# Expert layers of a two-block transformer: nine buffers for picked rows in place of eleven, and another place and moment for the last four query blocks

## The reference, cut to what matters

```python
def peer_ffn(x, norm_g, q_w, sub_keys, u, v):      # T = 256 tokens, D = 1024
    h = rmsnorm(x, norm_g).reshape(T, D)
    q = (h @ q_w).reshape(T, PEER_HEADS, 2, PEER_HALF)          # 8 heads, 2 halves of 128
    s = jnp.einsum('thcd,ckd->thck', q, sub_keys)               # 128 keys for each half
    s1, i1 = lax.top_k(s[:, :, 0], 16)
    s2, i2 = lax.top_k(s[:, :, 1], 16)
    # all 256 sums of pairs, the best 16, their expert numbers idx and softmax gates
    ...
    a = jnp.einsum('nd,nhkd->nhk', hb, u[ib])                   # each token: 8 heads x 16 experts
    w = gb * jax.nn.gelu(a, approximate=False)
    return jnp.einsum('nhk,nhkd->nd', w, v[ib])
```

## Time and profile before

| | us |
|---|---|
| median of 3 runs | 2757.41 |
| lowest, highest | 2756.09, 2761.15 |
| the profiled execution, its own time | 2753.48 |
| span of the profile (first to last instruction) | 2751.7 |
| POOL waits for PE ahead of gathers, whole span | 512.5 (319 waits) |
| DVE waits for gathers, whole span | 383.6 (314 waits) |

### The profile page before, as it was taken

How to read it: one execution, slowest core, us unless ns; L and a number is a source line. 1 busy time by engine, 2 the same in 40 slices (tenths; PEclk the granted TensorE clock), 3 DMA queues, 4 the chain that set the end, 5 groups by cost and what they waited for, 6 DMA issues and landing times.

```text
span 2751.7 us, 32201 instructions
## 1 busy us (share of the span) xinstructions
PE 2464.5 (90%) x10416; PEld 1675.6 (61%) x10416; DVE 1902.5 (69%) x3840; ACT 1178.2 (43%) x2586; POOL 857.9 (31%) x700
## 2 busy tenths in 40 slices
PE   8999999999899999998899777779888898787788
PEld 7888788888778878986444333334764444233234
DVE  7885588888668875655667767666567676766664
ACT  4446744544574456563333322333453333333334
POOL 0005400000230026664333333443433333333443
PEclk9999999999999999999999999889999999988999
DMA  6554355555425544448999999999549999999995
GB/s 212 188 177 138 128 194 186 180 191 184 148 90 189 190 153 138 154 153 353 419 416 418 417 418 409 418 413 395 178 153 419 419 419 418 413 419 415 413 415 239
DMA packets 141953, 783.39 MB, mean 285 GB/s; under 512 B 15873, under 2 KB 16385, under 8 KB 76289
## 3 DMA queue, kind: packets, MB, share of 16 engines
q0 software_dynamic: 73728, 536.90, 47.2%
q1 hardware_dynamic: 65360, 237.44, 25.7%
q10 hardware_dynamic: 2736, 7.46, 0.9%
HBM read 780.69 MB, written 1.05 MB: 284 GB/s over the span
## 4 chain that ended last, share of the span: by engine, by line
PE 47%; DMA 24%; DVE 9%; ACT 7%; issue 7%; POOL 6%; POOLq 0%; ACTq 0%; SPq 0%; DVEq 0%
DMA arena<-experts,arena 24%; PE ps L703 11%; PE ps L681 6%; PE ps L682 6%; PE ps L683 6%; PE ps L704 5%; PE ps L1283 5%; PE ps L1286 5%; POOL ring_lo L387 4%; DVE arena L2687 2%; POOL arena L2804 2%; ACT row L1887 2%; ACT arena L1880 1%; ACT L1878 1%; DVE ring_lo L387 1%
## 5 line engine op out<-in xcount | busy, mean ns | idle before, releaser
L2687 DVE SCALAR_TENSOR_TENSOR arena<-arena,ps 128x1024 f32<-128x1024 f32 x512 | 617.5, 1220 | 385.1 <-DMA arena<-experts,arena 383.6
L1283 PE MATMUL ps<-arena,row 128*128 128x512 f32 x1024 | 570.1, 640 | 207.5 <-ACT row L1887 207.5
L2804 POOL DMA_INDIRECT arena<-experts,arena x512 | 483.4, 944 | 772.2 <-PE ps L1286 512.5
L1286 PE MATMUL ps<-arena,row 128*128 128x512 f32 x1024 | 553.9, 623 | 0.0
L381 ACT ACTIVATE ring_hi<-ring 128x1024 fp32r<-128x1024 f32 x416 | 437.7, 1058 | 177.7 <-PE ps L683 140.3
L703 PE MATMUL ps<-hT,ring_hi 128*128 128x512 f32 x1408 | 503.4, 400 | 3.4 <-DVE hT L2208 3.2
L1283 PEld LDWEIGHTS ps<-arena,row 128*128 128x128 f32 x1024 | 197.5, 201 | 487.3 <-ACT row L1887 279.3
L387 POOL TENSOR_TENSOR ring_lo<-ring,ring_hi 128x1024 fp32r<-128x1024 f32 x143 | 346.3, 2432 | 282.3 <-ACT ring_hi L381 261.6
L704 PE MATMUL ps<-hT,ring_lo 128*128 128x256 f32 x1408 | 395.8, 281 | 0.0
L1286 PEld LDWEIGHTS ps<-arena,row 128*128 128x128 f32 x1024 | 206.7, 202 | 269.0 <-issue 269.0
L387 DVE TENSOR_TENSOR ring_lo<-ring,ring_hi 128x1024 fp32r<-128x1024 f32 x273 | 331.9, 1239 | 20.5 <-ACT ring_hi L381 19.9
(11 more groups left out here) (341 smaller groups left out, 3553.8 us busy)
## 6 DMA issues: line engine op xcount, KB each, us to landing
ring<-stream SPq DMA_DIRECT2D x424, 512.0 KB, 3.4
arena<-experts,arena POOLq DMA_INDIRECT x512, 13.2
row<-rows_in ACTq DMA_DIRECT2D x11, 512.0 KB, 4.9
arena<-stream SPq DMA_DIRECT2D x8, 512.0 KB, 5.0
queries_in_ring_hi<-stream SPq DMA_DIRECT2D x8, 512.0 KB, 6.2
queries_in_w<-stream SPq DMA_DIRECT2D x4, 512.0 KB, 7.5
queries_in_h_lo<-stream SPq DMA_DIRECT2D x4, 512.0 KB, 5.4
x<-x_in SPq DMA_DIRECT2D x1, 1024.0 KB, 4.8
```

The costliest lines, as they stand in the source:

```text
L1283: lower = pe.matmul(ps[:, 2 * tb, :], diag, v[:, 0:HALF], start=first, stop=end)
L1286: pe.matmul(ps[:, 2 * tb + 1, :], diag, v[:, HALF:D], start=first, stop=end)\
L2687: last = dve.scalar_tensor_tensor(u, u, 1.0, h, ALU.mult, ALU.mult, accum_out=R["a"][:, n % 2, k:k + 1])
L2804: pool.indirect_dma_start(R["held"][:, g % HELD, :], None, experts, bass.IndirectOffsetOnAxis(ap=idx[:, n % 2, k:k + 1], axis=0))\
```

## The change

The ring of buffers for picked rows has nine places in place of eleven; pick g then waits until pick g - 9 is freed. The two places given up hold 4096 elements, which is the size of four query blocks. A tensor `last_queries` of that size lies at the end of the arena, and query blocks 12 to 15 have their place there and no longer in `ring_hi`. SP issues their loads together with those of blocks 2 and 3, after the wait for the mixer's last output and ahead of blocks 4 to 7, and no longer behind these and behind the waits on `used`. The rest of the program is the same: the same picks, products and order on PE, DVE, ACT and POOL.

```diff
-HELD = 11
+HELD = 9
...
-                       ("held", (HELD, EXPERT)))
+                       ("held", (HELD, EXPERT)), ("queries", (SLOTS, BLK)))
...
-        queries_in_w, queries_in_ring_hi = plain("queries_in_w", w_at, 2, BLK), plain("queries_in_ring_hi", ring_hi_at, SLOTS, BLK)
+        queries_in_w = plain("queries_in_w", w_at, 2, BLK)
+        last_queries = region(SPACE - SLOTS * BLK, SLOTS, BLK)[0]
...
-            return queries_in_ring_hi[:, b % SLOTS, :]
+            return last_queries[:, m - 3 * SLOTS, :]
...
-                        for early in (2, 3):
+                        for early in (2, 3, *range(3 * SLOTS, SUBS)):
                             sp.dma_start(raw(b + early), stream[b + early]).then_inc(raw_loaded(b + early), 16)
-                    if m < SLOTS or m // SLOTS == 2:
+                    if m // SLOTS != 1:
                         b += 1
                         continue
-                    if m < 2 * SLOTS:
-                        who, own = SPLIT[b - 2 * SLOTS][1:]
-                        sp.wait_ge(lo_ready[who], own + 1)
-                    else:
-                        sp.wait_ge(used, AT[f"peer{l}_q"] - SLOTS + m % SLOTS + 1)
+                    who, own = SPLIT[b - 2 * SLOTS][1:]
+                    sp.wait_ge(lo_ready[who], own + 1)
```

## The result

The changed kernel takes 2808.07 us (median of four runs, 2799.28 to 2810.93) where the kernel before, run beside it, takes 2757.07 (2756.09 to 2761.15): ratio 1.0175, 95% interval 1.0163 to 1.0187, so 51 us slower. The forecast was slower, 2795, with 2773 to 2820 around it. Its sign and place hold; its sum is 13 us low, and that is the net of larger errors.

The account below looks back on a forecast made before the run. The gathers' DMA queue was taken to bound both expert layers. Late pick 9 +37, second-order waits +2, query loads -0.7 and sub-keys +1 gave +39, taken as +38: 2795 us, range 2773 to 2820.

Parts of the forecast that it names:

- What bounds the kernel: Both expert layers, 656 us each: gathers set the pace at 2.49 us a pick, and empty-queue time is lost for good.
- Part 1, which gather is late, and for whom: Expert layers: pick 0's release now lets pick 9 go, not pick 11; pick 9 is late in 24 units.
- Part 1, by how much pick 9 is late: Expert layers: with 7.5 us per landing, 1.27 us on average in late units; +37 us taken, bounds 13 and 43.
- prediction's own last sign: Expert layers: the forecast is wrong if pick 0's release to pick 9's landing is not about 7.5 us.
- Rival A: Expert layers: the queue's stock covers two fewer buffers, needing an empty-queue price under 5.3 us; 2757 us, chance 0.05.
- they follow at the full rate: Unit 4 of layer 0: picks 10 and 11 follow late pick 9 at 2.49 us each, adding no further loss.
- Part 2: Expert layers: second-order waits at pick 1 and PE's lower clock after stalls, 0 to 15 us together, counted as 2.
- rival C: Expert layers: PE's lower clock after stalls delays later picks, another 1 us in twenty-four units; 2819 us, chance 0.14.
- Part 3: SP's query loads: early landing gains 0.7 us; sub-keys possibly late in layer 1 cost +1, bounds 0 and 4.
- rival D: Start of layer 1: first gather late by 3 us, beside the forecast and inside its range, with no separate chance.
- the +1: Start of layer 1: sub-keys landing behind the early query loads delay the first gather, counted +1 us, bounds 0 and 4.
- Rival B: Expert layers: a landing into an empty queue takes 6.6 us, losing 13 to 20 us; 2770 to 2778 us, chance 0.14.

Follow-up runs that it names:

- e3: Kernel before with all eleven buffers, but pick 9 of every unit waits as if there were nine: 2784.9 us, ratio 1.0099.
- e4: Kernel before with ten buffers in place of eleven: 2762.8 us, ratio 1.0014.
- e7: Kernel before with eight buffers, query blocks where they were: 2927.5 us, ratio 1.0621.
- e8: Kernel before, unedited, profiled once more in a single execution: 2760.3 us.
- e1: Kernel before with nine buffers alone, query blocks 12 to 15 left in ring_hi and loaded as before: 2803.7 us, ratio 1.0169.
- e11: Changed kernel with a unit's gates worked out on DVE between the last two dots of group 0, not behind them: 2779.3 us, ratio 1.0069.
- e2: Changed kernel run again, unedited: 2806.9 us, ratio 1.0177.
- e9: Kernel before, eleven buffers, with the next unit's expert numbers made ahead of the dots of group 2: 2756.4 us, ratio 0.9993.

## Why the prediction was right, and where it wasn't

*What bounds the kernel.* Right. The gathers' queue sets both stretches; every microsecond of the loss is in them, and a loss in the queue is not made good.

*Part 1, which gather is late, and for whom.* Right, and the core of it. The release of pick 0 lets pick 9 go; 27 units are dry there (24 were forecast), none before. e3 shows it by that wait alone, e4 and e7 that the place moves with the ring.

*Part 1, by how much pick 9 is late.* Forecast +37, with bounds 13 and 43. Measured as idle engines, +30 in the stretches, and as longer intervals ahead of pick 9, +27; about 9 of these, in the first unit of each layer, go with the late first release that e8 shows in the kernel before as well. The inputs were off in two directions. A dry pick 9 is used 5.5 to 7.3 us after its issue, 6.2 on average: less than 7.5, and less than the lowest landing of the earlier trace rows. By the prediction's own last sign, a landing about 7.5 us after the release, this input was wrong. But the release comes later: from the start of the dot of pick 3 to the issue that waits for it, 9.7 us on average, against 8.6 in the profile before and 9.2 in the second one (e8). The two partly cancel, and that is luck: neither was foreseen.

The Trainium skill's estimate ("DMA: Bandwidth & Descriptors", the anatomy of one DMA on the gpsimd path) of 4.4 us was too low here as well: from the issue to the last packet of a dry pick 9 the trace has 5.6 us on average and 5.05 at least. Rival A, which needed that price, is refuted by the result and by e1.

*Part 1, "they follow at the full rate".* This is the step that failed. The gathers behind a dry one come 3.1, 2.9 and 2.7 us apart, not 2.49: 0.6 + 0.4 + 0.2 = 1.3 us in each of 27 units (with unrounded means), 35 us. It shows as packets that take longer, +26 us by the DMA shares, and for the rest as idle engines at the start of the dry gather. The prediction had it at nothing, though the earlier trace rows hinted at it: a first gather into a queue that had just emptied took 8.0 us, not 6.6.

*What was given back.* The longer intervals at picks 0 to 2 fell from 17 to 10 us. A unit whose pick 9 is late has its expert numbers in time for the next one; that is a reading, which no run takes apart. The prediction counted such a gain in no term.

*Part 2.* Counted 2. PE's clock did fall, from 0.94 and 0.95 to 0.92 and 0.91, and 18 units (15 before, 17 in e8) have a granted clock of 0.50 among the first four products of group 0, so rival C names something real. How much it feeds back is bounded and not shown: the release is 0.5 us later than in e8, and if all of that were the clock's, it would be 12 us in the 27 units, half of C's price of 24. In e11 the same ring with an earlier Gelu has ten such units.

*Part 3.* Right that it is small: e1 and e2 are 3.2 us apart, no more than their noise; the sub-keys are not late, so rival D is refuted and the +1 was 0.

*The sum.* In the two profiles the time from pick to pick over 2.49 us grew from 32 to 88: +27 ahead of pick 9, +35 at picks 10 to 12, -7 at picks 0 to 2, and 1 elsewhere. Forecast were 37, 0, 0 and 2. Rival B (13 to 20 us) had the price of the landing nearly right, and was still wrong in the sum, for want of the second term and of the later release.

## What to carry to other kernels

Count a ring of buffers by its worst moment, not by the median: how many transfers are queued when the slowest release of a period comes, times the time of one, against issue to first use. Here one buffer less cost 5 us, two 46 to 51, three 170. A queue that is empty for half a microsecond loses more than that, as the transfers behind it start slowly; and if a ring has to be short, an edit that brings the one slow release forward (e11: the gates one dot earlier) brings 29 us, over half of what the tenth buffer brings, while it is worth nothing in a ring that is long enough. And time gathers by when they land, not by when they start: e9 won 11 us at the first packets and nothing at the dots.

## What the runs showed of the hardware that was not expected

A queue of gathers that ran dry doesn't resume at its full rate. A packet of 8 KB takes 0.31 us in the full queue. The first sixteen of a gather that finds the queue empty take 0.65 us on average, in unit 10 mostly about 1.0; the first sixteen of the next gather 0.47, and of the one after 0.38; in the third gather behind the dry one it is 0.32. In e3, where POOL fills the queue at 1.24 us a gather, the next gather's first sixteen take 0.37 and all is as before from the second on. Packets of over 0.5 us number 288 in the kernel before and 1121 in the changed one, of 65,536. Whether this is the order in which the engines reach memory, the writing of the descriptors, or something else was not tried. It would take a run with a queue emptied on purpose and gathers of other sizes behind it.
